# Gate blocks moved inside retention and the mLSTM stage, norm logarithms grouped, the mLSTM means moved into the out-projection

## The reference, cut to what matters

```python
for l in range(2):
    u = rms(h) * norm_w[l]
    proj = u @ w_in[l]
    # retention: 4 heads, decayed causal scores, RMS over each head
    ret_out = _rms(scores_decayed(rq, rk) @ rv) * silu(rz)
    # difference attention: 4 heads, RMS over each head
    diff_out = _rms(a @ dv) * norm_w * (1 - lam_init) * silu(dz)
    # SSD (Mamba-2), one RMS over 512 columns
    ssd_out = _rms(y * silu(sz)) * ssd_norm_w
    # mLSTM: 4 heads
    hh = sigmoid(mo) * mlstm(mq, mk, mv, mg)      # causal, log-gated, divided by a denominator
    ml_out = _layernorm(hh) * mlstm_norm_w * silu(mz)   # mean and variance over each head
    mix = concatenate([ret_out, diff_out, ssd_out, ml_out])   # 2048 columns
    h = h + mix @ w_out[l]
```

## Time and profile before

| | us |
|---|---|
| median of 3 runs | 2831.53 |
| lowest, highest | 2822.37, 2834.43 |
| the profiled execution, its own time | 2828.33 |
| its span, first to last instruction | 2826.3 |

### The profile page before, as it was taken

One profiled execution on the slowest core, in us unless ns is written; L12 is line 12 of the kernel. 1 busy time (PEld: TensorE's weight loads), 2 busy tenths in 40 slices (PEclk: granted clock), 3 DMA queues, 4 the chain that ended last, 5 costly groups with the idle time before them and its releaser, 6 DMA issues.

```text
span 2826.3 us, 31321 instructions
## 1 busy us (share of the span) xinstructions
PE 2447.6 (87%) x12233; PEld 1850.0 (65%) x12233; DVE 1591.0 (56%) x2435; ACT 815.7 (29%) x1742; POOL 914.0 (32%) x944
## 2 busy tenths in 40 slices
PE   3968897779999898899699989997889997999788
PEld 2756675558977566677576756583667675658356
DVE  6785684663254665646634467645454546764543
ACT  2332213420012552333313352313311325231231
POOL 2874896489402448821200002103120000220210
PEclk7979898887698999899899989997899998999788
DMA  6430554036442004320121111130122110112011
GB/s 205 147 114 17 125 142 90 9 112 153 104 88 47 1 2 112 112 67 16 60 75 45 61 45 46 47 103 15 45 76 88 45 61 30 60 45 93 27 45 60
DMA packets 229157, 200.27 MB, mean 71 GB/s; under 512 B 86835, under 2 KB 213139, under 8 KB 228755
## 3 DMA queue, kind: packets, MB, share of 16 engines
q1 hardware_dynamic: 217491, 156.33, 19.8%
q0 software_dynamic: 11520, 41.95, 5.0%
HBM read 196.16 MB, written 2.10 MB: 70 GB/s over the span
## 4 chain that ended last, share of the span: by engine, by line
PE 59%; POOL 17%; DVE 14%; ACT 5%; issue 4%; DMA 0%; SPq 0%; DVEq 0%; ACTq 0%; POOLq 0%
PE bank L506 14%; PE bank L508 13%; PE bank L507 13%; POOL mix L2142 5%; POOL mix L2139 4%; PE bank L654 3%; PE bank L618 3%; DVE wring_parts L1445 2%; POOL mix L2145 2%; PE bank L632 2%; POOL mix L2126 2%; PE bank L816 1%; DVE whi_parts L1444 1%; DVE bank L1516 1%; PE bank L572 1%
## 5 line engine op out<-in xcount | busy, mean ns | idle before, releaser
L507 PE MATMUL bank<-h_parts,whi_parts 128*128 128x512 f32 (+2 forms) x1336 | 540.2, 404 | 0.0
L1445 DVE TENSOR_TENSOR wring_parts<-wring,whi_parts 128x2048 fp32r<-128x2048 f32 (+1 forms) x138 | 333.9, 2420 | 4.7
L1444 DVE CAST whi_parts<-wring 128x2048 fp32r<-128x2048 f32 (+1 forms) x138 | 197.4, 1430 | 225.8 <-PE bank L508 190.7
L507 PEld LDWEIGHTS bank<-h_parts,whi_parts 128*128 128x128 f32 (+2 forms) x1336 | 254.0, 190 | 70.9 <-issue 7.8
L506 PE MATMUL bank<-vt_parts,whi_parts 128*128 128x512 f32 (+2 forms) x472 | 198.1, 420 | 33.0 <-ACT rs L1123 12.4
L2142 POOL TENSOR_TENSOR mix<-mix 128x512 f32<-128x512 f32 (+1 forms) x160 | 219.1, 1370 | 12.5
L507 PE MATMUL bank<-mix_parts,whi_parts 128*128 128x512 f32 x512 | 206.9, 404 | 0.0
L506 PE MATMUL bank<-pt_parts,whi_parts 128*128 128x512 f32 x392 | 165.6, 422 | 35.3 <-DVE wring_parts L1445 20.3
L508 PE MATMUL bank<-vt_parts,wring_parts 128*128 128x512 f32 (+2 forms) x472 | 192.4, 408 | 0.0
L2139 POOL TENSOR_TENSOR mix<-mix,cond 128x1024 f32<-128x1024 f32 x80 | 160.3, 2004 | 4.9 <-DMA mix<-in_ada_w 3.2
L506 PE MATMUL bank<-mix_parts,whi_parts 128*128 128x512 f32 (+2 forms) x408 | 161.8, 397 | 0.0
(11 more groups left out here) (366 smaller groups left out, 5443.6 us busy)
## 6 DMA issues: line engine op xcount, KB each, us to landing
wring<-in_w_in SPq DMA_DIRECT2D x60, 1024.0 KB, 5.2
mix<-in_ada_w POOLq DMA_DIRECT2D x80, 512.0 KB, 4.6
wring<-in_w_out SPq DMA_DIRECT2D x16, 1024.0 KB, 5.1
wring<-in_mla_w_in SPq DMA_DIRECT2D x10, 1024.0 KB, 6.8
wring<-in_mla_w_out SPq DMA_DIRECT2D x8, 1024.0 KB, 5.1
wring<-in_swa_w_in SPq DMA_DIRECT2D x32, 256.0 KB, 4.6
wring<-in_nsa_w_in SPq DMA_DIRECT2D x32, 256.0 KB, 4.4
wring<-in_nsa_w_in SPq DMA_DIRECT2D x6, 1024.0 KB, 5.1
```

Of the source, the lines that this page charges most:

```text
L507: pe.matmul(bank, lh, rl, start=False, stop=False)
L1444: chain(dve.tensor_copy(high, whole))
L1445: dve.tensor_tensor(low, whole, high.bitcast(F32), ALU.subtract).then_inc(done, 1)
```

## The change

Four things are done, in the two layers of the second stack alone.

1. `rstds` replaces four calls of `rstd`: all four Ln, then all four Exp, each head into a tile of its own instead of `rs`. The waits for DVE between heads (`mixed`) go.
2. Retention: the four `ret_z` blocks go one by one into the head loop, each between a head's scores and the next head's scores. DVE's `gate` goes into its head loop as well.
3. mLSTM: the eight blocks of `ml_o` and `ml_z` go between the heads' steps. DVE splits their weights inside its head loop. ACT puts the z gates in `qb` instead of `pt`. The casts of mix chunks 0 to 11 can no longer be spread over the heads, since they write over `h`; they now come after the last block.
4. The means go into the out-projection, after the first 24 products, and use ring O (two banks) instead of V (three).

```diff
-            def out_proj(L, n_k, between=None):
+            def out_proj(L, n_k, between=None, midway=None):
+                            if midway and i == 0 and k == 0 and (j, c) == (0, 4):
+                                midway()
...
-                for g in range(2):
-                    in_blocks(L, ("ret_z", g), A, [(L, "gate", 2 * g + j) for j in range(2)])
...
                 for e in range(RET_H):
+                    if e % 2 == 0:
+                        slots = weights(L, ("ret_z", e // 2))
+                    block_of(A, (L, "gate", e), slots, e % 2, hk)
+                    if e % 2:
+                        used(A.filled((L, "gate", e)))
                     if e + 1 < RET_H:
                         ret_scores(e + 1)
                     ret_values(e)
...
-                for g in range(2):
-                    in_blocks(L, ("ml_o", g), A, [(L, "mo", 2 * g + j) for j in range(2)])
-                for g in range(2):
-                    in_blocks(L, ("ml_z", g), A, [(L, "gate", 12 + 2 * g + j) for j in range(2)])
...
                 log_rows("mseg", 0, ML_H, 2)
-                for e in range(ML_H):
-                    if e + 1 < ML_H:
-                        log_rows("mseg", e + 1, ML_H, 2)
-                    ml_scores(e)
-                    if e:
-                        ml_values(e - 1)
-                ml_values(ML_H - 1)
-                for e in range(ML_H):
-                    pe.wait_ge(*cnt(hv_ready))
-                    bank = open_bank(V, (L, "mean", e))
+                log_rows("mseg", 1, ML_H, 2)
+                ml_scores(0)
+                ml_gate(0)
+                ml_gate(1)
+                log_rows("mseg", 2, ML_H, 2)
+                ml_scores(1)
+                ml_gate(2)
+                ml_values(0)
+                ml_gate(3)
+                log_rows("mseg", 3, ML_H, 2)
+                ml_scores(2)
+                ml_gate(4)
+                ml_values(1)
+                ml_gate(5)
+                ml_scores(3)
+                ml_gate(6)
+                ml_values(2)
+                ml_gate(7)
+                ml_values(3)
...
+                out_proj(L, 2, ml_norms, ml_means)
...
+            def rstds(names, n, to):
+                for e, name in enumerate(names):
+                    act.wait_ge(*A.filled(("norm", name)))
+                    act.activation(to(e), A.take(("norm", name))[:, :], ACT.Ln, scale=1.0 / n, bias=epsc[:, 0:1]).then_inc(A.empty, 1)
+                for e, name in enumerate(names):
+                    act.wait_ge(*A.emptied(("norm", name)))
+                    act.activation(to(e), to(e), ACT.Exp, scale=-0.5).then_inc(rstd_ready, 1)
```

More of the change, by code:

```diff
@@ L1045, in ml_values, with ml_gate, ml_means @@
                     causal_values(bank, e, lambda j: ones[:, :], False, True).then_inc(V.full, 1)
-                log_rows("mseg", 0, ML_H, 2)
-                for e in range(ML_H):
-                    if e + 1 < ML_H:
-                        log_rows("mseg", e + 1, ML_H, 2)
-                    ml_scores(e)
-                    if e:
-                        ml_values(e - 1)
-                ml_values(ML_H - 1)
-                for e in range(ML_H):
-                    pe.wait_ge(*cnt(hv_ready))
-                    bank = open_bank(V, (L, "mean", e))
-                    pe.matmul(bank[:, :], ones[:, :], kb[:, 4 + e, :], start=True, stop=True).then_inc(V.full, 1)
+                slots = [None]
+                def ml_gate(b):
+                    name, key = (("ml_o", b // 2), (L, "mo", b)) if b < 4 else (("ml_z", b // 2 - 2), (L, "gate", 8 + b))
+                    if b % 2 == 0:
+                        slots[0] = weights(L, name)
+                    block_of(A, key, slots[0], b % 2, hk)
+                    if b % 2:
+                        used(A.filled(key))
+                log_rows("mseg", 0, ML_H, 2)
+                log_rows("mseg", 1, ML_H, 2)
[17 more added lines that the diff above has]
+                ml_values(3)
+                def ml_means():
+                    for e in range(ML_H):
+                        pe.wait_ge(*cnt(hv_ready))
+                        bank = open_bank(O, (L, "mean", e))
+                        pe.matmul(bank[:, :], ones[:, :], kb[:, 4 + e, :], start=True, stop=True).then_inc(O.full, 1)
                 def ml_norms():
@@ L1385, in _, with ml_gate, em @@
                         copy_out((L, ("mv", g), i), vt[:, i, 256 * g:256 * (g + 1)], lambda bank: bank[:, 0:256])
-                for b in range(4):
-                    act.wait_ge(*A.filled((L, "mo", b)))
-                    act.activation(kb[:, b, :], A.take((L, "mo", b))[:, :], ACT.Tanh, scale=0.5).then_inc(A.empty, 1)
-                for b in range(4):
-                    act.wait_ge(*A.filled((L, "gate", 12 + b)))
-                    bank = A.take((L, "gate", 12 + b))
-                    act.activation(pt[:, 0, b, :], bank[:, :], ACT.Copy)
-                    act.activation(pt[:, 1, b, :], bank[:, :], ACT.Tanh, scale=0.5).then_inc(A.empty, 1)
+                def ml_gate(b):
+                    if b < 4:
+                        act.wait_ge(*A.filled((L, "mo", b)))
+                        act.activation(kb[:, b, :], A.take((L, "mo", b))[:, :], ACT.Tanh, scale=0.5).then_inc(A.empty, 1)
+                    else:
+                        act.wait_ge(*A.filled((L, "gate", 8 + b)))
+                        bank = A.take((L, "gate", 8 + b))
+                        act.activation(qb[:, b - 4, :], bank[:, :], ACT.Copy)
+                        act.activation(qb[:, b, :], bank[:, :], ACT.Tanh, scale=0.5).then_inc(A.empty, 1)
+                def em(e):
+                    act.wait_ge(*A.filled((L, "em", e)))
+                    act.activation(aux[:, :], A.take((L, "em", e))[:, :], ACT.Exp, scale=-1.0).then_inc(A.empty, 1)
                 def inverse(e):
@@ L1401, in _ @@
                 exps("mseg", 0)
-                for e in range(ML_H):
-                    if e + 1 < ML_H:
-                        exps("mseg", e + 1)
-                    if e:
-                        inverse(e - 1)
-                    act.wait_ge(*A.filled((L, "em", e)))
-                    act.activation(aux[:, :], A.take((L, "em", e))[:, :], ACT.Exp, scale=-1.0).then_inc(A.empty, 1)
+                exps("mseg", 1)
+                ml_gate(0)
+                ml_gate(1)
+                exps("mseg", 2)
+                ml_gate(2)
+                em(0)
+                ml_gate(3)
+                exps("mseg", 3)
+                ml_gate(4)
+                inverse(0)
+                em(1)
+                ml_gate(5)
+                ml_gate(6)
+                inverse(1)
+                em(2)
+                ml_gate(7)
+                inverse(2)
+                em(3)
                 inverse(ML_H - 1)
@@ L1851, in _ @@
                 prepare(2)
-                for b in range(4):
-                    gate((L, "gate", b), mix[:, b, :])
                 dve.wait_ge(*cnt(cb_masked))
@@ L2002, in _ @@
                 conv_silu(7)
-                prepare(4)
-                dve.wait_ge(*A.emptied((L, "gate", 15)))
-                for b in range(4):
-                    chain(dve.scalar_tensor_tensor(out=mix[:, 12 + b, :], in0=pt[:, 1, b, :], scalar=1.0, in1=pt[:, 0, b, :],
-                                                   op0=ALU.add, op1=ALU.mult))
+                prepare(2)
                 dve.wait_ge(*V.filled((L, "mutok")))
```

49 lines of the change are left out of this document (27 added, 22 removed).

## The result

| | us |
|---|---|
| before, median of 4 runs | 2832.20 (2822.37 to 2834.43) |
| after, median of 4 runs | 2756.62 (2746.99 to 2760.62) |
| ratio | 0.9727, 95% interval 0.9708 to 0.9745 |
| profiled execution of after: its own time, its span | 2746.99, 2745.2 |

The change makes the kernel 75.6 us (2.7%) faster by the medians. The forecast was 2764 us with a range of 2738 to 2790. The profiled execution of the changed kernel is the fastest of its four, 9.6 us under their median. Against the profiled execution before it is 81.3 us faster, and 4.1 us of that lie ahead of layer 4, in code that is the same in both.

A forecast was written before the change was run, and what follows sets the result against it. PE, busy for 87% of the span, was taken to bound the kernel. Savings of 34 (mLSTM), 18 (retention) and 12 us (difference norm), 64 in all, take the profiled 2828.3 us to 2764, range 2738 to 2790.

The forecast's parts named there:

- mLSTM: mLSTM stretch: 20.5 + 9 + 4 - 16.5 = 17 us saved per layer, 34 in both.
- retention: Retention: waits for score products and ACT's second Ln go, one new wait comes; 10 us saved in layer 4, 8 in layer 5.
- difference norm: End of the difference attention: 3.1 us wait goes, DVE is free earlier; with the clock 6 us a layer, 12 in both.
- 6 from the clock: mLSTM, per layer: 9 us of low clock go with the waits, 3 us come back behind the third mean's wait.
- Head waits: Inside the mLSTM heads: PE's two long waits for DVE (8.5 and 7.4 us) go, covered by gate blocks.
- The third mean: mLSTM out-projection: PE newly waits 13.8 us for DVE's first subtraction, between 7.3 uncontended and 16.0 contended; 16.5 with cold clock.
- The tail of the norms: End of mLSTM: with grouped Ln and Exp, PE waits three times 0.5 us instead of 5.4 us; 4 us less.
- The new wait: Retention: head 0's fourth score waits for DVE, still splitting the second ret_z unit; 2.2 us.
- More is won: Rival (0.15): DVE reaches the third mean's subtraction uncontended, wait 7.3 us; 13 to 19 us more, about 2748 us.
- Late inside the heads: Rival (0.17): in mLSTM the ACT and DVE chain is late, PE waits at blocks and values; 2783 us.
- mLSTM gains nothing: Rival (0.06): ACT and DVE set the stage, waits come back at the means; 2805 us.
- not 53: Rival of a slower kernel (0.03): PE waits 53 us per layer at the third mean; 2842 us or more.

The follow-up runs named there:

- Run 5: The changed kernel with POOL filling the low parts of the mix chunks with a constant, reading nothing; 2739.08 us, one execution.
- Run 4: The changed kernel with DVE's four mean subtractions directly behind head 3's output, ahead of split, casts and gate products; 2722.62 us, ratio 0.9624.
- run 1: The kernel before with the grouped logarithms alone, no gate block or mean moved; 2795.09 us, ratio 0.9877.
- run 8: The changed kernel with a useless DVE multiplication ahead of chunk 15's cast, repeated four times in layer 4, once in layer 5; 2760.61 us, one execution.
- Run 7: On top of run 6, DVE splits the second ret_z unit behind head 0's score products, under the first gate block; 2715.53 us, ratio 0.9594.
- run 6: On top of Run 4, DVE instead of POOL makes the low parts of chunks 12 to 15; 2729.69 us, ratio 0.9635.

## Why the prediction was right, and where it was not

The time (2764 against 2756.6 us) and the main mechanisms held. The saving was sized less well: 64 us were forecast, and it is 75.6 by the medians. The time came closer than the saving because the forecast was counted from the profiled execution, 3.9 us under the median of the kernel before. By its own steps, with before less after in the two profiled executions:

| step | predicted, both layers | measured |
|---|---|---|
| mLSTM | 34 | 31.3 (15.7 + 15.6) |
| retention | 18 (10 + 8) | 19.6 (10.65 + 8.95) |
| difference norm | 12 | 14.1 |
| SSD, rest of the out-projection | 0 | 7.4 + 4.6 |
| the rest of the two layers | 0 | -0.6 |

That is 76.4 us in the two layers; another 4.9 lie in code that the change leaves alone.

Inside the mLSTM row two errors met. From the first product behind SSD to the wait for the residual, layer 4 takes 237.50 us before and 221.80 now, and PE is busy for 206.10 and 197.22 us of it. So 8.9 us came from the clock and 6.8 from waits. The prediction had 6 from the clock (9 less the 3 behind the third mean) and some 10.7 from waits (20.5 + 4 - 13.8). That its 17 lies so near 15.7 is luck in part.

**Head waits.** Right: both long ones are gone, every group of eight products of values takes 2.42 us at most, and no gate block waited for a split. The clock of the mLSTM stretch is 0.93, where "near 0.9" stood.

**The third mean.** Right, 13.5 us for 13.8, in both layers. The estimate was a choice between a walk through DVE's queue without contention, 7.3 us, and one with contention everywhere, 16.0. The reason given for it held: POOL stands still for 3.8 us in this stretch. Run 5 shows the lower end: without POOL's reads 8.5 us are left (four casts take 2.23 and not 1.5 us). How near the chosen value came is luck in part. Run 4 shows that without this order of DVE's queue 0.7 us of the wait are left. The cold clock behind it was put at 3 us and is 2.4, by PE's busy time in run 4.

**The tail of the norms.** This is the term that was mis-sized. It was to fall from 5.4 to 1.5 us and fell to 4.8. The pace of 1.9 us a head came from multiplications of 0.69 us, but POOL makes a low part of the head before at that time, and L2122 then takes 1.64; a head is 2.80 us (1973.91 less 1971.11, from the start of one first multiplication to the next). The prediction used rows 9 for contention at the means and forgot them here. In the kernel before, 0.69 us was right for this place, because the heads came 4.2 us apart; the grouping itself brought DVE's multiplication beside POOL's low part. Run 5 shows it: without POOL's reads a head takes 1.85 us, the 1.9 of the prediction, and 1.6 us of wait are left, its 1.5. The grouping is worth 1.0 us in the mLSTM stretch (run 1), not 4.

The Trainium skill (SBUF — State Buffer, "Who interferes with whom") calls the ports that DVE and GpSimd share an exclusive lock, and says that a DVE instruction with two SBUF inputs contends for them with a GpSimd instruction that reads SBUF, not with one that only writes it. The rows of the tail agree: L2122 takes 1.64 against 0.69 us beside a low part of 1.70 us on POOL. They agree for writes too: in run 5 DVE's first multiplication (L2120, two SBUF inputs) takes 0.74 us with a fill beside it, and 0.75 without.

**What was left out.** "The convolutions behind it are DVE's as before, so I count nothing more" was the step that failed for SSD, and the rest of the out-projection was not looked at. Both were shorter mostly by the clock: a wait at the end of one stretch slows the first products of the next. For the out-projection that is shown (0.59 against 1.00, runs 1 and 8). In SSD 1.5 of the 3.8 us of layer 4 are the first 240 products (57.74 before, 56.20 now); the other 2.3 lie in its heads (51.99 and 49.70 us), where PE is busy for 1.9 us less and the granted clock is 0.90 and not 0.84. What sets the clock there isn't settled: in runs 5 and 8 layer 5's SSD took 109.8 us again, its heads at a clock of 0.81, though it was entered at full clock.

**Retention and the difference norm.** The new wait was put at 2.2 us and is 1.6; but the prediction did not see that it would bring the first gate block down to a clock of 0.66, 2.6 us. Run 7 takes both away. The sum came out right because more clock was won than the 3 us put down: head 0's eight products of values took 4.05 us before and take 2.42 now, and so with the other heads, some 5 us. Over the whole of layer 4's retention PE is busy for 4.0 us less (101.89 and 97.89 us), the slow gate block included. The end of the difference norm runs at 1.00 now and ran at 0.86: 7.1 us saved for 6 predicted. No run parts the two gains that the prediction named there, the wait for ACT and the earlier split.

**The rivals.** "More is won" needed DVE uncontended, and it wasn't. "Late inside the heads" did not happen. "mLSTM gains nothing" fell with 31.3 us. The third mean cost 13.5 us and not 53. The chances have one slip: the forecast and the first two rivals make 0.91, and most of the third's 0.06 would bring that to about 0.95, not 0.92.

## What to carry to other kernels

When blocks are moved to cover waits, look at what each engine's queue holds at the end of the covered part: here DVE had four subtractions that PE waited for, and did 13 us of other work first; putting them first was worth 28 us more (2722.6 us), and one split moved under a block brought the best time, 2715.5 us. Price every DVE instruction that may run beside POOL's reads by rows in which both are at work, at each place and not only at the one that looks critical, and ask whether the change itself brings the two together. And when a wait goes, count the clock of the untouched work behind it too: of 76 us, 7.6 came from there for certain (2.2 and 2.4 in the out-projection, twice 1.5 in SSD), and 12 at the most.

## What the runs showed of the hardware that was not expected

- A single wait of 1.6 us on PE, behind 2.2 us of score products that use 64 rows, was followed by 12 products at the lower clock (the block took 8.4 us); without the wait (run 7) none was. Behind the same wait in layer 5 the block took 7.3 us. In run 8 a wait of 2.4 us between products of the out-projection was followed by full clock, and one of 4.8 us by 0.72 in the next 6 us.
- DVE's multiplication of two SBUF tiles takes 0.69 us alone and 1.64 beside POOL's subtraction; beside a fill the one at hand (L2120) takes 0.74 us and 0.75 without. Four casts take 2.23 us beside fills of 2.7 us and 3.56 beside subtractions of 5.8 us.
- A low part takes 0.69 us on DVE (run 6). On POOL it takes 1.27 us when DVE does nothing beside it (2011.85 us, before) and 1.70 beside DVE's multiplications, which lose 0.95 us each.
